# Two norms taken from one pair of sums between two blocks, with one operand's half made earlier

## The reference

```
h = h + _conv_ffn(_rmsnorm(h, ffn_norm_w[l]), ffn_up[l], ffn_conv_w[l], ffn_down[l])
return _rmsnorm(h, final_norm_w)
...
m = jax.nn.silu(cvec) @ w_mod + b_mod
...
def modulated_norm(x, g, shift, scale):
    return rms_norm(x, g) * (1 + scale) + shift
...
x = ffn_half_step(x, mx[0:3], g_ffn1[l], w_ffn1_gu[l], w_ffn1_down[l])
if ctx_live:
    ctx = ffn_half_step(ctx, mc[0:3], g_ffn1[l], w_ffn1_gu[l], w_ffn1_down[l])
```

## Time and profile before

| what | value |
|---|---|
| time, 3 runs | 2305.45, 2306.55, 2307.18 us (median 2306.55) |
| profiled execution | 2307.5 us, of which the span in the trace is 2305.3 |
| PE busy | 2147.1 us, 93% of the span |
| DVE, ACT, POOL busy | 1012.2, 788.8, 238.8 us |
| chain that ended last, by engine | PE 83%, DVE 8%, ACT 3%, DMA 3%, issue 2% |
| mean granted TensorE clock | 0.967 |

### The profile page before, as it was taken

One profiled execution on the slowest core, in us unless ns is written; L12 is line 12 of the kernel. 1 busy time (PEld: TensorE's weight loads), 2 busy tenths in 40 slices (PEclk: granted clock), 3 DMA queues, 4 the chain that ended last, 5 costly groups with the idle time before them and its releaser, 6 DMA issues.

```text
span 2305.3 us, 31344 instructions
## 1 busy us (share of the span) xinstructions
PE 2147.1 (93%) x13697; PEld 1817.9 (79%) x13698; DVE 1012.2 (44%) x1286; ACT 788.8 (34%) x968; POOL 238.8 (10%) x207
## 2 busy tenths in 40 slices
PE   6987699999989999989889999999999998988997
PEld 5974398899868888868668888776887886858997
DVE  6664654676652232242452232234222224645454
ACT  5631244454443223233233222223322223444443
POOL 1000300122201001110001101110100111001101
PEclk9997799999999999999999999999999999999999
DMA  6325643445562232243242232234224223353453
GB/s 224 144 84 211 237 147 147 170 169 186 190 238 80 78 126 77 88 171 110 92 164 92 65 127 92 87 135 181 80 90 168 85 86 108 110 216 132 170 190 107
DMA packets 53544, 314.23 MB, mean 136 GB/s; under 512 B 5920, under 2 KB 11936, under 8 KB 23584
## 3 DMA queue, kind: packets, MB, share of 16 engines
q1 hardware_dynamic: 51216, 309.48, 38.0%
q10 hardware_dynamic: 2192, 2.75, 0.4%
HBM read 311.16 MB, written 1.05 MB: 135 GB/s over the span
## 4 chain that ended last, share of the span: by engine, by line
PE 83%; DVE 8%; ACT 3%; DMA 3%; issue 2%; SPq 0%; POOL 0%; ACTq 0%; DVEq 0%
PE psum L236 25%; PE psum L238 25%; PE psum L237 25%; DMA raw<-in_mod 3%; PE psum L1519 2%; DVE w_lo L220 2%; ACT w_hi L212 2%; PE psum L1224 1%; PE psum L1202 1%; DVE work L387 1%; PE psum L326 1%; PE psum L1216 0%; DVE xc L1372 0%; PE psum L1619 0%; PE psum L1620 0%
## 5 line engine op out<-in xcount | busy, mean ns | idle before, releaser
L236 PE MATMUL psum<-xn_hi,w_hi 128*128 128x256 f32 (+1 forms) x2504 | 846.6, 338 | 35.2 <-DVE xn_lo L380 16.4
L237 PE MATMUL psum<-xn_lo,w_hi 128*128 128x256 f32 (+1 forms) x2504 | 840.8, 336 | 0.0
L238 PE MATMUL psum<-xn_hi,w_lo 128*128 128x256 f32 (+1 forms) x2504 | 840.0, 335 | 0.0
L220 DVE TENSOR_TENSOR w_lo<-raw,w_hi 128x2048 fp32r<-128x2048 f32 (+1 forms) x246 | 507.8, 2064 | 459.5 <-ACT w_hi L212 459.0
L236 PEld LDWEIGHTS psum<-xn_hi,w_hi 128*128 128x128 f32 x2504 | 482.1, 193 | 93.0 <-issue 43.0
L237 PEld LDWEIGHTS psum<-xn_lo,w_hi 128*128 128x128 f32 x2504 | 482.2, 193 | 47.3 <-issue 0.7
L238 PEld LDWEIGHTS psum<-xn_hi,w_lo 128*128 128x128 f32 x2504 | 481.7, 192 | 47.1
L212 ACT ACTIVATE w_hi<-raw 128x2048 fp32r<-128x2048 f32 (+1 forms) x246 | 421.7, 1714 | 193.7 <-PE psum L238 170.0
L236 PE MATMUL psum<-h_hi,w_hi 128*128 128x512 f32 (+1 forms) x880 | 307.1, 349 | 3.6 <-POOL h_lo L1494 3.6
L237 PE MATMUL psum<-h_lo,w_hi 128*128 128x512 f32 (+1 forms) x880 | 306.5, 348 | 0.0
L238 PE MATMUL psum<-h_hi,w_lo 128*128 128x512 f32 (+1 forms) x880 | 306.5, 348 | 0.0
(11 more groups left out here) (335 smaller groups left out, 1388.8 us busy)
## 6 DMA issues: line engine op xcount, KB each, us to landing
raw<-in_mod SPq DMA_DIRECT2D x72, 1024.0 KB, 4.8
raw<-in_a_up SPq DMA_DIRECT2D x42, 1024.0 KB, 4.8
raw<-in_b_up SPq DMA_DIRECT2D x42, 1024.0 KB, 4.8
raw<-in_ffn_up SPq DMA_DIRECT2D x22, 1024.0 KB, 4.9
raw<-in_a_down SPq DMA_DIRECT2D x32, 704.0 KB, 4.2
raw<-in_b_down SPq DMA_DIRECT2D x32, 704.0 KB, 4.1
raw<-in_ffn_down SPq DMA_DIRECT2D x16, 704.0 KB, 4.1
raw<-in_wo SPq DMA_DIRECT2D x8, 1024.0 KB, 4.9
```

The source lines that it names most:

```text
L220: dve.tensor_tensor(w_lo[:, slot, 0:size], raw[:, raw_slot(("main", g)), 0:size], w_hi[:, slot, 0:size].bitcast(F32), ALU.subtract).then_i ...
L236: pe.matmul(out, lh, rh, start=first, stop=False, skip_group_check=group)
L237: pe.matmul(out, lh, rl, start=False, stop=False, skip_group_check=group)
L238: return pe.matmul(out, ll, rh, start=False, stop=last, skip_group_check=group)
```

## The change

`between` goes as a norm of its own. `n20` becomes a `FinalNorm` over the tokens: in each last down step of `feed0` ACT squares the tile twice, once with `final_norm_w` as a scale, into the two halves of a 512-wide `nrm`. One set of sums gives both mean squares, and DVE forms both reciprocal roots in one 512-wide pass. `joint` is the product of the gains of both norms. Once the tiles for `feed1` are written, DVE writes the final-normed residual back to `xc` (`dve_residual`). PE waits for all eight weighted squares before it starts these sums.

The context's half becomes `n20c`, a `ContextNorm`. Its squares come between up and down of `feed0`'s first half, its sums and statistics between the halves, and its tiles are scaled and split one in each down step of the second half, in between the chunk splits.

The mods are dealt out anew: 4 ahead of `feed0` (3 before), 3 between its halves (none before), 5 ahead of `feed1` (9 before, in two lots). `branch_act` issues its six transfers behind the norm instead of ahead of it. `act_squares_after` is now passed by the callers, `dve_scaled` is cut in two functions, and the rest keeps its order.

```diff
-MODS_DURING = dict(w_out=24, ffn_up0=3, a1_up0=9, ab_a=3, ab_out=4, a2_up0=5, a2_down1=3, b1_up0=5, b1_up1=4, wo2=12)
+MODS_DURING = dict(w_out=24, ffn_up0=4, ffn_up1=3, a1_up0=5, ab_a=3, ab_out=4, a2_up0=5, a2_down1=3, b1_up0=5, b1_up1=4, wo2=12)
...
-            def act(self, act, then):
+            def act(self, act, then, before_down=None, halfway=None):
 
                 for half in range(2):
+                    if half and halfway is not None:
+                        halfway()
...
                     run_act(act, job, evac, splits=self.conv is None)
-                    run_act(act, jobs[f"{self.name}_down{half}"], then.act_squares_after(act) if half else None)
-
-            def dve(self, dve, halfway=None, late=None):
+                    if not half and before_down is not None:
+                        before_down()
+                    run_act(act, jobs[f"{self.name}_down{half}"], then if half else None)
+
+            def dve(self, dve, halfway=None, late=None, beside_down=None):
...
-                    run_dve(dve, jobs[f"{self.name}_down{half}"], dve_add_gated(dve, 1, self.gate, self.w // T))
-
-            def pool(self, pool):
+                    add = dve_add_gated(dve, 1, self.gate, self.w // T)
+
+                    def add_and(s):
+                        add(s)
+                        if half and beside_down is not None:
+                            beside_down(s)
+                    run_dve(dve, jobs[f"{self.name}_down{half}"], add_and)
...
+        class ContextNorm(Norm):
+            def dst(self, k, t):
+                return area(4096, KT, T)[:, k, t]
+            def act_squares(self, act):
+                act.wait_ge(ctx_in, 16)
+                act.wait_ge(n_lo, ffn.split_base + KT)
+                for k in range(0, KT, self.tiles):
+                    act.activation(nrm[:, k:k + self.tiles, 0:T], xc[:, k:k + self.tiles, C], ACT.Square).then_inc(n_sq, 1)
+        class FinalNorm(Norm):
+            def __init__(self, scale, shift):
+                super().__init__(X, scale, shift)
+                self.w = 2 * T
+            def act_squares_after(self, act, also):
+                def evac(s):
+                    act.wait_ge(evacuated, s.g + 1)
+                    act.activation(nrm[:, s.c, 0:T], xc[:, s.c, X], ACT.Square, scale=col("final_norm_w", s.c)).then_inc(final_sq, 1)
+                    act.activation(nrm[:, s.c, T:2 * T], xc[:, s.c, X], ACT.Square).then_inc(n_sq, 1)
+                    also(s)
+                return evac
+            def dve_stats(self, dve):
+                m, r, j3 = mean[:, :], rstd[:, :], 3 * self.j
+                tmp = work[:, 7168:7168 + 2 * T]
+                dve.wait_ge(n_sum, self.j + 1)
+                dve.tensor_scalar(m[:, C], psum[:, 6, C], 1.0 / D, EPS, ALU.mult, ALU.add).then_inc(final_mean, 1)
+                dve.wait_ge(final_mean, 1)
+                dve.scalar_tensor_tensor(m[:, X], m[:, C], D * EPS, psum[:, 6, X], ALU.mult, ALU.add).then_inc(n_mean, 1)
+                dve.wait_ge(n_mean, self.j + 1)
+                dve.wait_ge(n_guess, self.j + 1)
+                dve.scalar_tensor_tensor(tmp, r, -0.5, r, ALU.mult, ALU.mult).then_inc(n_rstd, 1)
+                dve.wait_ge(n_rstd, j3 + 1)
+                dve.tensor_tensor(tmp, tmp, m, ALU.mult).then_inc(n_rstd, 1)
+                dve.wait_ge(n_rstd, j3 + 2)
+                dve.scalar_tensor_tensor(r, tmp, 1.5, r, ALU.add, ALU.mult).then_inc(n_rstd, 1)
+                dve.wait_ge(n_rstd, j3 + 3)
+            def dve_residual(self, dve):
+                for k in range(KT):
+                    dve.scalar_tensor_tensor(xc[:, k, X], xc[:, k, X], col("final_norm_w", k), rstd[:, C], ALU.mult, ALU.mult).then_inc(final_x, 1)
+        final_sq, final_mean, final_x, final_scale = (sem(x) for x in ("final_squares", "final_mean", "final_residual", "final_scale"))
+        joint = small[:, cols["joint"]:cols["joint"] + KT]
+        def final_gains(dve):
+            w = small[:, cols["final_norm_w"]:cols["final_norm_w"] + KT]
+            dve.scalar_tensor_tensor(joint, scales[:, 0, :, 0], D ** 0.5, w, ALU.mult, ALU.mult).then_inc(final_scale, 1)
+            dve.wait_ge(final_scale, 1)
...
         def branch_act(act, norm, then):
+            norm.act_rest(act)
             for name in L0_TABLES:
                 act.dma_start(L0_TABLES[name][:], io[name]).then_inc(l0_tables_in, 16)
-            norm.act_rest(act)
...
-        between = Norm(X, lambda k, h: col("final_norm_w", k), out=xc[:, :, X])
-        n20, n21 = modulated(0, XC, direct=5), modulated(1, XC)
+        n20c = ContextNorm(C, lambda k, h: scales[:, 0, k, 1:2], lambda k, h: mods[:, k, 1:2], tiles=4, direct=4)
+        n20 = FinalNorm(lambda k, h: col("joint", k), lambda k, h: mods[:, k, 0:1])
+        n21 = modulated(1, XC)
...
-            mods_pe(pe, 3)
-            feed0.pe(pe)
-            between.pe(pe)
             mods_pe(pe, 4)
+
+            def context_sums():
+                n20c.pe(pe)
+                mods_pe(pe, 3)
+            feed0.pe(pe, context_sums)
+            pe.wait_ge(final_sq, KT)
             n20.pe(pe)
             mods_pe(pe, 5)
...
-            feed0.act(act, between)
-            between.act_rest(act)
-            act.wait_ge(ctx_in, 16)
-            for k in range(KT):
-                act.wait_ge(n_scaled, between.scaled_base + k + 1)
-                act.activation(nrm[:, k, :], xc[:, k, :], ACT.Square).then_inc(n_sq, 1)
+            def context_high(s):
+                n20c.act_high(act, range(s.c, s.c + 1))
+            feed0.act(act, n20.act_squares_after(act, context_high), lambda: n20c.act_squares(act), lambda: n20c.act_guess(act))
             n20.act_rest(act)
...
-            feed0.dve(dve)
-            between.dve(dve)
+            def context_stats():
+                n20c.dve_stats(dve)
+                final_gains(dve)
+
+            def context_tile(s):
+                if s.c == 0:
+                    dve.wait_ge(ff_lo, feed0.bases[1] + HALF)
+                n20c.dve_scale(dve, s.c)
+                if s.c:
+                    n20c.dve_low(dve, s.c - 1)
+            feed0.dve(dve, context_stats, None, context_tile)
+            n20c.dve_low(dve, KT - 1)
             n20.dve(dve)
+            n20.dve_residual(dve)
+            dve.wait_ge(final_x, KT)
             mod_rows_out(dve)
...
-            feed0.pool(pool)
-            between.pool(pool)
+            feed0.pool(pool, lambda: n20c.pool(pool))
             n20.pool(pool)
```

More of the change, by code:

```diff
@@ L398, in pool_lows @@
                                        ALU.subtract).then_inc(n_lo, 1)
+            def dst(self, k, t):
+                return nrm[:, k, t] if self.out is None else self.out[:, k, t]
             def ready(self, pe, k):
@@ L1995, in _ @@
             n25.act_rest(act)
-            feed4.act(act, last)
+            feed4.act(act, last.act_squares_after(act))
             last.act_rest(act)
```

51 lines of the change are left out of this document (28 added, 23 removed).

## The result

| what | value |
|---|---|
| before, 7 runs | median 2306.55 us (2304.20 to 2308.28) |
| changed, 7 runs | median 2314.19 us (2313.39 to 2316.48) |
| ratio, changed to before | 1.0026, 95% interval 1.0014 to 1.0037 |
| span of the profiled execution | 2314.7 us (before 2305.3) |
| mean granted clock | 0.965 (before 0.967) |

The forecast was 2311.3, with a range to 2317, and slower as the likeliest case. The change is slower by 0.26%, 6 us by the ratio and 7.6 by the two medians.

What follows compares the result with a forecast made beforehand. PE, busy 93% of the span, was the bound, so its stops decide. +6.35 + 1.3 + 2.6 - 5.3 - 2.2 + 2 = +4.7 us gave an execution of 2312.2, median 0.95 lower: 2311.3, range 2304.5 to 2317.

Steps and rivals of the forecast that it cites:

- The bound: Whole kernel: PE is busy 93% of the span, so only its stops matter; a mod, not a norm, ends last before `feed1`.
- Between the halves, +6.35: New PE stop between `feed0`'s halves for sums and three mods, the third waiting for its transfer: 6.35 us.
- The second table, +1.3: First up step of `feed0`'s second half: Silu's table must be fetched again on ACT, costing PE 1.3 us.
- Rival 4: Between `feed0`'s halves: ACT stands as long again behind the refetched table, another 1.28 us, 2312.6; chance 1 in 20.
- The fourth mod, +2.6: Ahead of `feed0`: waiting for its load delays PE's start by 3.2 us, less 0.6 in the first step: +2.6.
- The end of `feed0`, -5.3: Last down steps to `feed1`: ACT's operations delay the last square, but fewer mods follow; `feed1` starts 5.3 us sooner.
- `branch_act`, -2.2: At its norm: with the transfers behind it, PE starts 2.2 us sooner, or 1.1 if the clock stays low.
- The clock, +2: PE's new stops around `feed0` and in `feed1`'s first step may cost half-speed stretches: +2 us, between 0 and 5.
- 1: `feed0`'s end: ACT's extra operations hide in its idle time, -12.4 instead of -5.3 us, 2304.2 or 2301.2; chance 0.13.
- 2: Around `feed0` and `branch_act`: landings are slow and the clock falls at each stop, +13 us, 2319.6; chance 0.1.
- 3: The edit in `branch_act` does nothing, if weights and not the norm hold PE there: +2.2 us, 2313.5; inside forecast's range.

Runs made afterwards that it cites:

- e6: The kernel before with only the mods dealt as in the change (4 ahead of `feed0`, 3 between its halves, 5 behind), both norms kept; ratio to before 1.0040.
- e2: The changed kernel with the mods dealt as before (3 ahead of `feed0`, none between its halves, 9 behind); ratio to before 1.0050.
- e3: The changed kernel with DVE's add and context's tile ahead of its next chunk's split in `feed0`'s second down steps; ratio to before 0.9992.
- e7: The changed kernel with the context's tiles scaled and split behind `feed0` instead of one in each down step; ratio to before 1.0008.
- e1: The changed kernel with the six table transfers put ahead of the norm in `branch_act` again; ratio to before 1.0053.
- e10: The changed kernel with `joint` 16 columns wide instead of 8, tiles behind `small` moved by 64 bytes; ratio to before 0.9990.
- e5: The kernel before with only the six table transfers put behind the norm in `branch_act`; ratio to before 0.9996.
- e9: The kernel before with only eight unused columns more in the tile `small` (32 bytes); ratio to before 1.0013.
- e12: The kernel before with only 32 unused columns more in the tile `small` (128 bytes); ratio to before 0.9971.
- e11: The kernel e8 with `joint` 16 columns wide instead of 8, tiles behind `small` moved by 64 bytes; ratio to before 0.9950.
- e4: The changed kernel with one mod taken back from ahead of `feed0` (3, 3 and 6 instead of 4, 3 and 5); ratio to before 1.0025.
- e8: The changed kernel with e3's order and mods in small lots: 3 ahead of `feed0`, 2 ahead of each half's down steps, 2 between, 3 behind; ratio to before 0.9976.

## Why the prediction was right, point by point, and what it missed

**The bound.** That PE's stops decide, and that the last thing ahead of `feed1` is a mod and not the norm, held: 665.68 waits for its transfer, and `feed1` follows without idle time.

**Between the halves, +6.35.** From 538.41 to the mod's end at 545.02 are 6.6 us. Sums 2.25, third mod's wait 1.35, as worked out. The clock did not fall here; in e6, in a stop of the same length, it did (at 542). That all of mid grew by 7.6, the 6.35 + 1.3 of my sum, is in part luck: stop and table are 6.6 + 1.5, and the down steps ahead of them took 33.3 us in place of 33.8. Their slower passes added 1.2, and a stretch at half clock that before had at 506, worth 1.6, was not there.

**The second table, +1.3.** PE idles 1.46 us at 558.17, behind the load at 553.66. e2, which has sums and table but no mods there, pays 3.1 us against the 3.5 of my two terms (2.2 + 1.3). Rival 4's pause is not there: the Trainium skill ("ScalarE: Activation LUTs", section "What ACT_TABLE_LOAD costs") adds a drain to each switch, and here the load takes 1.28 us (653.51) and ACT's next operation starts 0.01 us behind it, at 654.80.

**The fourth mod, +2.6.** It costs 3.1 us where the clock stays up (A in e3 and e7, 20.8 against 17.6) and 5.8 where it falls (the changed kernel, e1, e6, e10). The mechanism was right. The 0.6 us that I took off for the first step was too much: I had priced an up step at the pace of down passes, 5.4 us, and it takes 5.85. The clock's share, 2.7, was in the clock's term at 2 with a chance of one in two.

**The end of `feed0`, -5.3.** The row of reasons held: three short operations in each turn, the last square late, PE's 8 us stand, sums at half clock, two transfers end on end. From PE's last down pass (ended at 644.75) to `feed1` are 22.8 us, "about 22" in the prediction, and 27.4 before. The chain's step was 4.52 where I had 4.36: the weighted square adds 0.42 us to each turn (636.34 to 636.76) and the shifted copy 0.40 (637.07 to 637.47), and not 0.32 each. PE also lost 1.5 us in the down steps, not 0.4: 1.2 by its slower passes, and the rest by waiting. The stretch as a whole gave 3.0. Against e5 and e9, which have the kernel before's code there, it would be 6.2 and 6.8. In both the clock fell in the sums, in e5 from those of `between` on, as PE's rows in e5_before_tables_last show:

```profile
636.56 0.79 PE L326 MATMUL psum<-work,ones 128*128 128x256 f32 x1 [3.39 <-ACT work L310]
...
647.48 1.06 PE L326 MATMUL psum<-work,ones 128*128 128x512 f32 x1
```

Ten passes of sums take 5.16 us there and 4.46 in the earlier trace rows. So the same code gives 70 us (before, e12) or 73 (e5, e9), and my 5.3 lies between the two gains.

**`branch_act`, -2.2, or -1.1 if the clock stayed low for as long from its fall.** PE's wait is 3.76 us, not 5.94, as the first said. But in this execution the low clock reaches over 6 us of its work and not 4, so about 1.1 is given back, as the lower bound had it. That is not so each time: PE's first 40 passes there take 12.0 us in the changed kernel and 11.0 before, but 10.5 to 10.8 in e2, e5, e7, e10 and e11, which have the same order of transfers and keep the whole gain.

**The clock, +2.** Some 2.7 in A, nothing between the halves, 1 in `branch_act`: 3.7, inside my 0 to 5.

**Missed: the layout.** The step that failed is a silent one, "the rest keeps its order", so that I set everything behind `branch_act` at nothing. The tail cost 2.7 us, and e9 shows that the eight columns alone do 2.4 of it. By the paces above, 264 passes of 5.0 ns more are an estimated 1.3 us in each 256-wide half, 5.3 in the four, the halves of `feed0` included; there some of it hides, as PE waits for the last square less (2.61 us in e9, 3.39 before).

**The number, and luck.** The terms as measured in the profiles are +5.8, +7.6, -3.0, -0.5 and +2.7, which is +12.5 and far more than the +4.7 of the sum. The sum had A too good by 3.2, the end by 2.3 and `branch_act` by 1.7, and lacked the tail's 2.7; its clock term of 2 covers part of that. Against them stand -3.2 over stretches that no edit touches: -0.6 ahead of the sums of `ffn`, and -1.4 and -1.2 in two later ones. That leaves +9.4 between the two profiled spans, and over all runs 6 us by the ratio. So the direction and the waits were foreseen, but that the time came out within 3 us of the forecast is in part luck.

**The rivals.** 1 fell by the 4.52 us step, and e3 shows what it would have been. 2 came in half: the clock fell at two of its places, and the third mod landed as forecast. 3 fell by PE's wait, though e1 and the changed kernel don't differ over the whole stretch. 4 fell by the row at 653.51.

**What stays open.** What in the address of an operand sets the pace of a pass, and why one half of e5 ran slower at before's addresses; which shift is best; whether the merged norm gains anything by itself; why e4's ratio does not show its A; and how much of the 0.13% of e9, whose interval holds 1, is its layout beyond the tail.

## What to carry to other kernels

When an edit adds an operation to a stage in which two engines take turns, price the turn and not the engine's idle time, and try first to reorder one queue so that the turns come apart: here that took 7.4 us off the end of `feed0`. A load moved out of a row of waits waits again where it lands (2.90, 1.35, 2.51 and 2.33 us here), unless the ring has room there, as for e8's two mods between the halves. And a change that resizes any tile in front of others must be compared at equal addresses, or its time is partly its layout's: add unused columns to the old kernel, and try a few widths on the new one.

## What the runs showed of the hardware

- PE's passes on an operand followed one another every 113.3 to 120.0 ns (256 wide) and 226.7 to 233.3 ns (512 wide) by where its tile lay, moved by 0, 32, 64 or 128 bytes, with all instructions the same; in the kernel before this was worth from +0.13% (32 bytes, interval 0.9998 to 1.0028, so perhaps nothing) to -0.29% (128 bytes, 0.9951 to 0.9990). One half of e5 left the pace of its layout, 117.8 ns for 113.4. The Trainium skill ("SBUF — State Buffer", section "Operand start alignment") gives start rules for an operand and says that they are about legality, not speed. These runs show that the address bears on speed too.
- With the same code the clock fell or stayed behind the same stop: at the start of `feed0` (A 20.8 or 23.4 us) and in the sums of `n20` (end 70 or 73 us). One such fall is worth about 3 us, half of what was to be measured. Behind the norm in `branch_act`, with the same instructions there, PE's first 40 passes took 12.0 us in the changed kernel and 10.8 in e2.
- A function table's load took 1.28 us on ACT, and the next operation stood right behind it (653.51 and 654.80 in the changed kernel).
